# Second layer's convolution projection issued by token tile inside the combination of the first layer, with its weights and eight modulation pieces moved in the DMA queue

## The chip, the cores and the metric

The kernel runs on one core of a Trainium2 chip. The metric is the device time of one execution in microseconds (us); the time before is the median of three runs. A core has TensorE (PE in the profile, its weight loads PEld), VectorE (DVE), ScalarE (ACT), GpSimd (POOL) and SyncE (SP), which here issues nearly all large transfers; its queue is SPq. Each engine works through its own program in order, and they meet through semaphores.

## The reference, cut to what matters

Two layers of one trunk run on 640 tokens of 1024 float32 channels: 512 sample tokens and 128 prompt tokens, each group with its own conditioning vector. What touches the change:

```python
def adaln(cvec, w, b):                      # w is 1024 x 6144 for each layer
    m = jax.nn.silu(cvec) @ w + b
    return [part[:, None, :] for part in jnp.split(m, N_MOD, axis=-1)]

def trunk_layer(x, mods, n1, n2, mix_p, kf, attend, moe_p):
    sh1, sc1, g1, sh2, sc2, g2 = mods
    h = rmsnorm(x, n1) * (1 + sc1) + sh1
    y, k, v = token_mixers(h, *mix_p, kf, attend)   # h @ w_in, four mixers, @ w_out
    x = x + g1 * y
    h = rmsnorm(x, n2) * (1 + sc2) + sh2
    x = x + g2 * hier_moe(h, *moe_p)                # 32 experts, top 2 for each token
    return x, k, v
```

The first 512 columns of `w_in` feed the Conformer convolution: `a * sigmoid(g)` of the two halves, then a depthwise filter of 31 taps. Everything is float32.

## The kernel before, in words

**Tiles.** Tokens are cut into NT = 5 tiles of P = 128 (four of the sample, one of the prompt). `X` holds the tokens by row; `hT` holds the modulated, normalised tokens by channel, as KC = 8 blocks of 128 channels by 640 tokens. PSUM is `ps`, eight banks of 512 columns. Weights pass through `ring`, six slots of 1 MB; slots 0 to 3 are counted by `w_full`, slots 4 and 5 by `a_full`. Three more units of 1 MB, `inv_s`, `mix_s` and `fwd_s`, hold tables for the mixers and expert weights in the mixture.

**Order of a layer.** On PE: convolution projection (L1060 to L1094: four blocks of 128 output columns in the order 2, 0, 3, 1, each 8 matmul pairs, L1076 over the 512 sample tokens into bank m and L1077 over the 128 prompt tokens into bank 4), Fourier and attention projections, Hyena, then the output projection (L1310 to L1336: ten groups n = 0 to 9 of 8 matmuls of 512 columns at L1318, two for each token tile, with the transposes and the router of the tile before between them), routing, and the experts: NSTAT = 28 blocks in a written-out loop, then a loop of blocks that the router decides (`turns` turns of SLOTS = 2). A block is one expert on up to 64 rows: gather, gate and up (L1370), hidden (L1377), down (L1385), gate by DVE, scatter.

**Combination.** After the experts SP waits for the last scatters (L750) and reads the two expert rows of every token back from `y_scratch`, one transfer of 1 MB for each tile (the first in two halves, L755 to L758). DVE adds them to `X` (L2306, L2324, semaphore `x_new`). If a layer follows, ACT takes the sum of squares and the root (`statistics`, L1477 and L1479), DVE the reciprocal (`root`, L1806), ACT writes the scaled rows (`scaled_rows`, L1472), PE transposes them with 8 instructions (`columns_of_x`, L1031) and ACT and DVE modulate half of the blocks each into `hT` (`modulate`, L1487 and L1814). Before, PE does this for all five tiles (L1454 to L1461) and only then, with `h_act` and `h_dve` complete for the last tile, starts the convolution projection.

**Modulation pieces.** The product `silu(c) @ ada_w` comes in 24 pieces of 1 MB for each layer. `ada_piece(p)` is the transfer by SP (L579); `ada(p)` is PE's part, four matmuls of 512 columns into bank 5 (L940). `apos` gives the place of each piece; a transfer waits until the piece before it in the same place has been used (`a_free`, semaphore `a_used`). Eight pieces make a set; set 1 of the second layer is pieces 32 to 39. Its transfers 32 to 35 stand between those of the combination, 36 and 37 behind the convolution weights, 38 and 39 after the next two input weights; PE takes 32 to 37 between the tiles of the combination and 38 and 39 inside the projection. The result is read at the start of the second layer: ACT copies it (`ada_rows(1, 1)`, L1495), DVE adds the gate row (`gate_row`, L1832) behind the third tap of the convolution.

**After the projection.** ACT takes the sigmoid of blocks 2 and 3 (L1584 and, for the prompt tokens, L1590), DVE multiplies (L1954, L1957, semaphore `cv_glu`) and runs the 31 taps (L1972). PE goes on with the Fourier projection (L1103) when `cv_glu` is complete.

**SP's order around the change.** In the first layer: ... `gate_up_next(2)` after `a_used` reaches 32, wait for `wo_mm` 10 (the last group of the output projection), weights of the experts 0 and 1, then one gate/up and one down transfer for each block as its slot comes free; a loop for the blocks beyond the 28th; the combination's reads; `in_unit(1, 0)` and `in_unit(1, 1)` (L596), which are the two 1 MB halves of the second layer's convolution weights, into `ring` slots 0 and 1.

Of the kernel before, what the change touches and what calls it, by code (L numbers as in the profile page):

```python
# [12 lines left out]
P = 128  # L13
D = 1024
KC = D // P
# [84 lines left out]
def trunk(nc, io, out):  # L100
    ctx = ExitStack()
    with ctx:
# [150 lines left out]
        def kept(*dims):  # L253
# [212 lines left out]
            (cv_mm, 4), (cv_sig, 3), (cv_glu, 2), (cv_tap, 2 * TAPS),  # L466
# [24 lines left out]
        def w_count(l, j):  # L491
            return 16 * (2 + 3 * l + j // 4) + 16 * ((j % 4 == 3) * l + (j == OUT_U + 3)) + l * 32 * uses(0, gu_units, j % 4, NSTAT) \
                + 16 * l * apos[32:40].count(j % 4)
# [20 lines left out]
        def dn_count(l, n):  # L514
# [4 lines left out]
        apos = [(4, 5, 0, 1, 2, 3)[p] if p < 6 else (4, 6)[p % 2] if 24 <= p < 32 or p >= 40 else 2 + p % 2 if p in (34, 35)  # L519
                else 4 + p % 2 for p in range(24 * DEPTH)]  # L520
# [7 lines left out]
        def a_count(p):  # L528
            if p >= 32 and apos[p] < 4:
                return w_count(1, apos[p]) - 16 - 16 * apos[p:40].count(apos[p]) + 16  # L530
            return 16 * (len([n for n in range(p) if min(apos[n], 5) == min(apos[p], 5)]) + 1)
# [38 lines left out]
        def _(sp):  # L570
# [11 lines left out]
            def in_unit(l, j):  # L582
                lo, n, k0, k1 = {0: (0, 512, 0, 4), 1: (0, 512, 4, 8), 2: (1280, 256, 0, 8), 3: (1536, 512, 0, 4),
                                 4: (1536, 512, 4, 8), 5: (512, 256, 0, 8), 6: (768, 256, 0, 8), 7: (1024, 256, 0, 8)}[j]
                if j in (4, 5):
                    sp.wait_ge(cv_mm, nth(l, cv_mm, 4))
# [6 lines left out]
                elif j in (2, 3):  # L593
                    sp.wait_ge(a_used, 33 + j)
# [44 lines left out]
            for l in range(DEPTH):  # L639
# [7 lines left out]
                if l > 0:  # L647
                    ada_piece(38)
                    ada_piece(39)
# [63 lines left out]
                if l:  # L713
                    down_next(2)
                sp.wait_ge(wo_mm, nth(l, wo_mm, 10))
# [14 lines left out]
                for n in range(NSTAT + SLOTS - ahead_d):  # L730
# [6 lines left out]
                    down_next(n + ahead_d)  # L737
                with sp.Fori(1, turns) as j:
# [14 lines left out]
                for t in range(NT):  # L753
# [173 lines left out]
        def _(pe):  # L927
# [1425 lines left out]
```

## Time and profile before

| what | value |
|---|---|
| time of the runs | 1508.46, 1508.89, 1510.42 us; median 1508.89 us |
| span of the profiled execution, first to last instruction | 1502.3 us |
| its own time | not listed apart from the three; against the median 6.6 us lie around the span |
| PE busy | 1253.7 us, 83% of the span |
| DVE, ACT, POOL busy | 660.0, 330.3, 260.5 us |
| chain that ended last | PE 63%, DMA 15%, DVE 13%, issue 4%, ACT 3% |
| moved by DMA | 357.42 MB, mean 238 GB/s |
| mean granted clock of PE | 0.932 of full |

The span is what the instructions of the profile cover; the time of a run has the start and the end of the program around it. Times of rows are us from the span's start. "Busy" of PE is a modelled length of each matmul, of which neighbours overlap, so the distance between the starts of two rows says more than their lengths. A matmul in float32 appears as two instructions. The chain of waits follows the work that ended last back to what released it.

### The profile page before, as it was taken

Reading aid. Unit: us, or ns where it says so; the run is one execution under the profiler, and the core shown is the slowest. Engines: PE = TensorE matmul, PEld = TensorE weight load, DVE = VectorE, ACT = ScalarE, POOL = GpSimd, SP = SyncE. Lnnn points to the kernel's source line nnn. Section 1 sums busy time; section 2 is a strip of 40 time slices with the busy share of each in tenths; the row PEclk is TensorE's granted clock in tenths of the full one; section 3 lists DMA queues with packets and bytes.
Section 4 is the critical chain, followed back from the end, with each engine's and each line's share of the span. In section 5 each row is a group of like instructions: output and inputs, shape, how many; then the busy total and the mean of one; then the engine's idle time right before and its main releaser. Section 6 shows DMA issues by size and latency. Waiting matters only on the chain.

```text
span 1502.3 us, 17089 instructions
## 1 busy us (share of the span) xinstructions
PE 1253.7 (83%) x6582; PEld 733.0 (49%) x6582; DVE 660.0 (44%) x1402; ACT 330.3 (22%) x663; POOL 260.5 (17%) x265
## 2 busy tenths in 40 slices
PE   3899998988996889998873989898899688888871
PEld 1456474455554445554441466544645544444440
DVE  3327456365245443443335087454723533323235
ACT  4411124310431111111115011442023211111112
POOL 4210110001001233332320017000000023322220
PEclk9999999999995999999996999999999689999996
DMA  9747330063025999999978431214421669999985
GB/s 350 279 175 259 140 109 28 29 214 141 15 107 198 381 372 419 417 406 402 381 313 353 179 112 29 81 33 141 170 91 43 266 239 419 418 416 419 418 333 220
DMA packets 74099, 357.42 MB, mean 238 GB/s; under 512 B 13262, under 2 KB 22092, under 8 KB 38825
## 3 DMA queue, kind: packets, MB, share of 16 engines
q1 hardware_dynamic: 58588, 323.30, 55.5%
q0 software_dynamic: 12704, 22.03, 4.0%
q10 hardware_dynamic: 2732, 11.08, 1.9%
q8 instruction: 49, 0.80, 0.2%
q14 instruction: 26, 0.21, 0.0%
HBM read 339.27 MB, written 31.23 MB: 247 GB/s over the span
## 4 chain that ended last, share of the span: by engine, by line
PE 63%; DMA 15%; DVE 13%; issue 4%; ACT 3%; POOL 1%; SPq 1%; ACTq 0%; POOLq 0%; DVEq 0%
PE ps L1370 11%; PE ps L1318 9%; PE ps L1385 8%; PE ps L1171 5%; DMA work<-h_scratch,tabs 4%; PE ps L1076 4%; DMA ring<-in_ada_w 4%; PE ps L1132 3%; DMA mix_s<-in_exp_up 2%; PE ps L1103 2%; PE ps L940 2%; PE ps L1377 1%; PE ps L993 1%; DMA work<-y_scratch 1%; PE ps L1178 1%
## 5 line engine op out<-in xcount | busy, mean ns | idle before, releaser
L1370 PE MATMUL ps<-ring,work 128*64 128x256 f32 x1312 | 158.6, 397 | 5.0 <-DMA ring<-in_exp_up 3.4
L1385 PE MATMUL ps<-ring,work 128*64 128x512 f32 x456 | 122.6, 661 | 33.2 <-DVE work L2249 19.1
L1318 PE MATMUL ps<-ring,yT 128*128 128x512 f32 x320 | 140.3, 593 | 1.0 <-DVE yT L2095 1.0
L1370 PEld LDWEIGHTS ps<-ring,work 128*64 128x64 f32 x1312 | 102.6, 145 | 75.6 <-issue 31.5
L873 POOL DMA_INDIRECT y_scratch<-work,tabs x56 | 68.1, 1216 | 311.2 <-DVE work L2255 311.2
L868 POOL DMA_INDIRECT work<-h_scratch,tabs x60 | 62.5, 1041 | 304.8 <-DVE tabs L2229 279.1
L2255 DVE TENSOR_TENSOR work<-ps,yT 128x512 f32<-128x512 f32 x56 | 38.7, 691 | 141.0 <-PE ps L1385 141.0
L1972 DVE SCALAR_TENSOR_TENSOR work<-work,prmT 128x655 f32<-128x655 f32 x120 | 97.8, 894 | 0.0
L1318 PEld LDWEIGHTS ps<-ring,yT 128*128 128x128 f32 x320 | 59.5, 190 | 70.3 <-issue 68.4
L1171 PE MATMUL ps<-hT,ring 128*128 128x512 f32 x192 | 88.6, 604 | 1.1 <-DVE ring L1989 1.1
L1739 ACT ACTIVATE work<-ps 64x256 f32<-64x256 f32 x56 | 21.0, 375 | 298.7 <-PE ps L1370 298.6
L1370 PE MATMUL ps<-inv_s,work 128*64 128x256 f32 x320 | 72.4, 379 | 3.1 <-DMA mix_s<-in_exp_up 3.1
L1370 PE MATMUL ps<-mix_s,work 128*64 128x256 f32 x320 | 72.5, 380 | 0.0
L2247 DVE TENSOR_TENSOR work<-work,ps 64x256 f32<-64x256 f32 x56 | 23.8, 425 | 108.6 <-ACT work L1739 108.2
L1076 PE MATMUL ps<-hT,ring 128*128 128x512 f32 x128 | 67.4, 609 | 1.7 <-POOL hT L839 1.7
L1385 PEld LDWEIGHTS ps<-ring,work 128*64 128x64 f32 x456 | 30.5, 144 | 76.4 <-issue 45.4
L1731 ACT ACTIVATE work<-ps 128x512 f32<-128x512 f32 x70 | 41.8, 597 | 91.7 <-PE ps L1361 91.7
L940 PE MATMUL ps<-ring,c_act 128*32 128x512 f32 x320 | 47.0, 671 | 16.7 <-DMA ring<-in_ada_w 16.5
L1370 PEld LDWEIGHTS ps<-inv_s,work 128*64 128x64 f32 x320 | 43.9, 138 | 34.1 <-issue 16.4
L847 POOL TENSOR_TENSOR yT<-yT 128x512 f32<-128x512 f32 x4 | 31.7, 7923 | 162.5 <-ACT yT L1601 162.5
L1361 PE MATMUL ps<-sq,work 128*128 128x128 f32 x280 | 46.1, 288 | 13.3 <-DMA work<-h_scratch,tabs 11.9
L2103 DVE TENSOR_TENSOR work<-ps,work 128x512 f32<-128x512 f32 x20 | 13.8, 691 | 95.9 <-PE ps L1318 95.9
(386 smaller groups left out, 2050.4 us busy)
## 6 DMA issues: line engine op xcount, KB each, us to landing
ring<-in_exp_down SPq DMA_DIRECT2D x57, 1024.0 KB, 12.9
ring<-in_exp_gate SPq DMA_DIRECT2D x41, 1024.0 KB, 9.7
ring<-in_exp_up SPq DMA_DIRECT2D x41, 1024.0 KB, 14.1
ring<-in_ada_w SPq DMA_DIRECT2D x40, 1024.0 KB, 7.7
inv_s<-in_exp_gate SPq DMA_DIRECT2D x20, 1024.0 KB, 9.3
mix_s<-in_exp_up SPq DMA_DIRECT2D x20, 1024.0 KB, 15.0
ring<-in_w_in SPq DMA_DIRECT2D x16, 1024.0 KB, 8.4
fwd_s<-in_exp_down SPq DMA_DIRECT2D x11, 1024.0 KB, 18.6
```

The costliest lines, as they stand in the source:

```text
L868: pool.indirect_dma_start(xg[:, s, :], None, H_half, bass.IndirectOffsetOnAxis(ap=rows.bitcast(U32), axis=0), bounds_check=2 * T - 1, oob_ ...
L873: pool.indirect_dma_start(Y_half, bass.IndirectOffsetOnAxis(ap=rows.bitcast(U32), axis=0), ye[:, s, :], None, bounds_check=2 * T * TOPK - ...
L940: last = mm(ps[32 * g:32 * g + 32, 5, :], c_act[:, k, :], w[:, 512 * g:512 * g + 512], start=(k == 0), stop=(k == KC - 1))
L1076: mm(ps[:, m, :], lhs, hT[:, k, 0:LS], start=(k == 0), stop=(k == KC - 1))
L1132: mm(ps[:, bank, :], lhs, hT[:, k, 0:LS], start=(k == 0), stop=(k == KC - 1))
L1171: last = mm(ps[:, 7, :], wh[m // 2][:, k, m % 2 * P:(m % 2 + 1) * P], hT[:, k, 0:LS], start=(k == 0), stop=(k == KC - 1))
L1318: last = mm(ps[:, (4, 6, 7, 0)[n % 4], :], yT[:, k, t * P:(t + 1) * P], wo[k // 2][:, k % 2, h * HALF:(h + 1) * HALF], start=(k == 0), sto ...
L1361: last = tr(ps[:, 0, k * P:(k + 1) * P], xg[:, s, k * P:(k + 1) * P], ident)
L1370: last = mm(ps[BR * q:BR * q + BR, 1, 0:FE], xe[:, s, kb, BR * h:BR * h + BR], w[q][:, k, :], start=(k == 0), stop=(k == KC - 1))
L1385: last = mm(ps[BR * h:BR * h + BR, 3, :], he[:, s, k, :], wd[:, k, HALF * h:HALF * h + HALF], start=(k == 0), stop=(k == 1))
L1731: return A(xe[:, s, :, :], ps[:, 0, :].rearrange("p (k t) -> p k t", k=4), ACT.Copy)
L1972: V.scalar_tensor_tensor(out=acc[:, c, :], in0=glu[:, c, j:j + CONV], scalar=prmT[:, c, j:j + 1], in1=acc[:, c, :], op0=ALU.mult, op1=ALU. ...
```

## The change

The second layer's convolution projection is done by token tile. For each tile PE does the transposes, and after the transposes of the next tile the 32 products of that tile (4 blocks of output columns by 8 of channels) over 128 tokens each. The combination's transposes use banks 6 and 7 in place of 0 to 3. On ACT and DVE, modulation of a tile and its reciprocal stand in another order. The convolution weights are asked for before the loop of the blocks that the router decides. Pieces 32 to 39 are asked for when the first layer's Hyena output is complete (`hy_zn`) and used in the first layer's output projection, one behind each group 1 to 8. The routing weights' PSUM bank goes from 5 to 6, as bank 5 now holds the set. `cv_mm` counts to 5.

```diff
-        apos = [(4, 5, 0, 1, 2, 3)[p] if p < 6 else (4, 6)[p % 2] if 24 <= p < 32 or p >= 40 else 2 + p % 2 if p in (34, 35)
-                else 4 + p % 2 for p in range(24 * DEPTH)]
+        apos = [(4, 5, 0, 1, 2, 3)[p] if p < 6 else (4, 6)[p % 2] if 24 <= p < 32 or p >= 40 else 4 + p % 2 for p in range(24 * DEPTH)]
...
                 if j in (4, 5):
-                    sp.wait_ge(cv_mm, nth(l, cv_mm, 4))
+                    sp.wait_ge(cv_mm, nth(l, cv_mm, 5))
                 elif j == 6:
                     sp.wait_ge(fo_x, nth(l, fo_x, 5))
                 elif j == 7:
                     sp.wait_ge(at_mm, nth(l, at_mm, 5))
                 elif l == 0:
                     sp.wait_ge(a_used, 3 + j)
-                elif j in (2, 3):
-                    sp.wait_ge(a_used, 33 + j)
...
                 if l > 0:
-                    ada_piece(38)
-                    ada_piece(39)
                     table(mix_s, "mix_s", tab_in)
                     table(inv_s, "inv_s", tab_in)
...
                 gate_up_next(2)
                 if l:
                     down_next(2)
+                else:
+                    sp.wait_ge(hy_zn, nth(l, hy_zn, 4))
+                    for p in range(32, 40):
+                        ada_piece(p)
                 sp.wait_ge(wo_mm, nth(l, wo_mm, 10))
                 gate_up_next(0)
...
                     down_next(n + ahead_d)
+                if l + 1 < DEPTH:
+                    sp.wait_ge(g_mm, NSTAT)
+                    in_unit(l + 1, 0)
+                    in_unit(l + 1, 1)
                 with sp.Fori(1, turns) as j:
...
                     sp.dma_start(ycomb[t].rearrange("p k d -> p (k d)"), yrow[t]).then_inc(yc_in[t], 16)
-                    if l + 1 < DEPTH and t:
-                        ada_piece(31 + t)
-                if l + 1 < DEPTH:
-                    in_unit(l + 1, 0)
-                    in_unit(l + 1, 1)
-                    ada_piece(36)
-                    ada_piece(37)
...
+                wc = [wbuf(CONV_U + h, 4, 512) for h in range(2)]
+
+                def conv_tile(t):
+
+                    for n, m in enumerate((2, 0, 3, 1)):
+                        for k in range(KC):
+                            dst = ps[:, m, t * P:(t + 1) * P] if t < NT - 1 else ps[:, 4, m * P:(m + 1) * P]
+                            last = mm(dst, wc[k // 4][:, k % 4, m * P:(m + 1) * P], hT[:, k, t * P:(t + 1) * P],
+                                      start=(k == 0), stop=(k == KC - 1))
+                        if t == NT - 2 or t == NT - 1 and n == 3:
+                            last.then_inc(cv_mm, 1)
+
+                def tile_modulated(t):
+
+                    pe.wait_ge(h_act, norm_event(l, 0, t + 1))
+                    pe.wait_ge(h_dve, norm_event(l, 0, t + 1))
+
                 if l:
-                    pe.wait_ge(h_act, norm_event(l, 0, NT))
-                    pe.wait_ge(h_dve, norm_event(l, 0, NT))
+                    columns_of_x(l, 0, 0, (6, 7))
+                    pe.wait_ge(w_full[0], w_count(l, CONV_U))
+                    pe.wait_ge(w_full[1], w_count(l, CONV_U + 1))
+                    for t in range(1, NT):
+                        tile_modulated(t - 1)
+                        columns_of_x(l, 0, t, (6, 7))
+                        conv_tile(t - 1)
+                    tile_modulated(NT - 1)
+                    conv_tile(NT - 1)
                 else:
                     pe.wait_ge(mods_ok, 3)
-                pe.wait_ge(w_full[0], w_count(l, CONV_U))
-                pe.wait_ge(w_full[1], w_count(l, CONV_U + 1))
-                wc = [wbuf(CONV_U + h, 4, 512) for h in range(2)]
-                for c in range(2):
+                    pe.wait_ge(w_full[0], w_count(l, CONV_U))
...
-                            elif l and k == KC - 1 and place in (3, 7):
-                                ada(38 + place // 4)
...
                         if l and n == 0:
                             ada_columns(1, 2)
+                        if l == 0 and 1 <= n <= 8:
+                            ada(31 + n)
                         if h == 0 and t >= 1:
...
-                    for t in range(NT):
-                        e = norm_event(l + 1, 0, t)
-                        if t >= 2:
-                            pe.wait_ge(h_act, e - 1)
-                            pe.wait_ge(h_dve, e - 1)
-                        columns_of_x(l + 1, 0, t, ((0, 1), (2, 3))[t % 2])
-                        for p in ((), (32,), (33, 34), (35,), (36, 37))[t]:
-                            ada(p)
 
...
-                for t in range(NT + 2):
-                    if l + 1 < DEPTH and 1 <= t <= NT:
-                        scaled_rows(l + 1, 0, t - 1)
-                    if l + 1 < DEPTH and t >= 2:
-                        modulate(l + 1, 0, t - 2, (0, 2)[t % 2])
+                for t in range(NT + 1):
                     if t < NT:
                         act.wait_ge(x_new, nth(l, x_new, t + 1))
                         statistics(l + 1, 0, t, ycomb[t][:, 1, :])
+                    if l + 1 < DEPTH and t:
+                        modulate(l + 1, 0, t - 1, 6)
+                    if l + 1 < DEPTH and t < NT:
+                        scaled_rows(l + 1, 0, t)
 
...
-                    if l + 1 < DEPTH:
-                        if 1 <= t <= NT:
-                            root(l + 1, 0, t - 1).then_inc(st_dg, 1)
-                        if t >= 2:
-                            modulate(l + 1, 0, t - 2, (1, 3)[t % 2])
-                    elif t >= 2:
+                    if l + 1 == DEPTH and t >= 2:
...
                         V.tensor_tensor(X[:, t, :], X[:, t, :], ycomb[t][:, 1, :], ALU.add).then_inc(x_new, 1)
+                    if l + 1 < DEPTH and 1 <= t <= NT:
+                        modulate(l + 1, 0, t - 1, 7)
+                    if l + 1 < DEPTH and t < NT:
+                        root(l + 1, 0, t).then_inc(st_dg, 1)
```

## Rows read from the trace of the kernel before

**Rows 1.** The chain of waits, 780 to 960: start, length, what held it (times in us).
```profile
768.76 11.62 DMA mix_s<-in_exp_up
...
789.86 2.11 DMA y_scratch<-work,icol
...
795.95 14.83 DMA work<-y_scratch
...
815.55 14.26 DMA ring<-in_ada_w
...
831.79 1.74 PE ps L1076 x2
...
869.77 0.38 DVE work L1954
```

**Rows 2.** Busy time by stretch: PE, PEld, DVE, ACT, POOL, granted clock, DMA share, GB/s.
```profile
361.00:445.00 84.00, 83.28 (x292) 44.59 (x292) 25.76 (x73) 24.69 (x43) 6.10 (x12) 1.00 0.15 53
...
802.00:831.70 29.70, 17.31 (x88) 7.61 (x88) 15.36 (x39) 19.42 (x38) 0.00 (x0) 0.61 1.03 407
831.70:869.80 38.10, 37.97 (x148) 20.21 (x144) 0.72 (x2) 1.88 (x4) 0.00 (x0) 0.98 0.31 125
...
737.00:780.00 43.00, 34.52 (x238) 18.23 (x234) 13.60 (x30) 4.86 (x10) 11.82 (x20) 1.00 0.99 408
724.00:737.00 13.00, 11.28 (x88) 6.78 (x86) 5.17 (x12) 1.94 (x4) 4.74 (x8) 1.00 0.93 336
```

**Rows 3.** Instructions in order, 786 to 833: start, length, engine, line [idle before, releaser].
```profile
797.96 1.23 DVE L2324 TENSOR_TENSOR X<-X,work 128x1024 f32<-128x1024 f32 x1 [1.05 <-DMA work<-y_scratch]
...
800.40 0.29 ACT L1479 ACTIVATE stat<-stat,epsc 128x1 f32<-128x1 f32 x1
800.86 1.23 DVE L2306 TENSOR_TENSOR X<-X,work 128x1024 f32<-128x1024 f32 x1 [1.68 <-DMA work<-y_scratch]
...
802.20 1.15 ACT L1472 ACTIVATE work<-X,stat 128x1024 f32<-128x1024 f32 x1 [1.50 <-DVE stat L1806]
...
803.49 1.94 PE L1031 MATMUL ps<-sq,work 128*128 128x128 f32 x8 [15.53 <-ACT work L1472]
...
805.84 1.23 DVE L2306 TENSOR_TENSOR X<-X,work 128x1024 f32<-128x1024 f32 x1 [2.50 <-DMA work<-y_scratch]
...
808.23 1.48 ACT L1487 ACTIVATE hT<-ps,mods,gain 128x128 f32<-128x128 f32 x4
...
810.80 1.22 DVE L2306 TENSOR_TENSOR X<-X,work 128x1024 f32<-128x1024 f32 x1 [1.27 <-DMA work<-y_scratch]
...
815.77 1.23 DVE L2306 TENSOR_TENSOR X<-X,yT 128x1024 f32<-128x1024 f32 x1 [1.27 <-DMA yT<-y_scratch]
...
818.40 1.06 PE L1031 MATMUL ps<-sq,work 128*128 128x128 f32 x8 [2.04 <-DVE hT L1814]
...
824.51 1.36 DVE L1814 TENSOR_SCALAR hT<-ps,gain,mods 128x128 f32<-128x128 f32 x4 [2.04 <-PE ps L1031]
```

**Rows 4.** PE's instructions in order, first layer's output projection.
```profile
361.89 20.77 PE L1318 MATMUL ps<-ring,yT 128*128 128x512 f32 x48
```

**Rows 5.** PE's instructions in order, 838 to 843.7, old convolution projection.
```profile
840.08 1.02 PE L1076 MATMUL ps<-hT,ring 128*128 128x512 f32 x2
840.94 0.38 PE L1077 MATMUL ps<-hT,ring 128*128 128x128 f32 x2
841.25 1.07 PE L940 MATMUL ps<-ring,c_act 128*32 128x512 f32 x8
842.25 1.12 PE L1076 MATMUL ps<-hT,ring 128*128 128x512 f32 x2
```

**Rows 6.** Transfers issued from 750 to 1000: size, median us from issue to landing.
```profile
ring<-in_ada_w SPq DMA_DIRECT2D x9, 1024.0 KB, 13.5
```

**Rows 7.** SP's instructions in order, 655 to 800.
```profile
714.35 9.70 SPq L696 DMA_DIRECT2D ring<-in_exp_down  x2
```

**Rows 8.** Line L1139, second layer: duration in ns, first and last start.
```profile
L1139 PE MATMUL ps<-ring,hT x64: 275/275/276, 925.6 to 932.6; 128*128 128x128 f32 x64
```

More of the change, by code:

```diff
@@ L1060, in _ @@
             for l in range(DEPTH):
-                if l:
-                    pe.wait_ge(h_act, norm_event(l, 0, NT))
-                    pe.wait_ge(h_dve, norm_event(l, 0, NT))
+                wc = [wbuf(CONV_U + h, 4, 512) for h in range(2)]
[10 more added lines that the diff above has]
+                    pe.wait_ge(h_dve, norm_event(l, 0, t + 1))
+                if l:
+                    columns_of_x(l, 0, 0, (6, 7))
[7 more added lines that the diff above has]
+                    conv_tile(NT - 1)
                 else:
                     pe.wait_ge(mods_ok, 3)
-                pe.wait_ge(w_full[0], w_count(l, CONV_U))
-                pe.wait_ge(w_full[1], w_count(l, CONV_U + 1))
-                wc = [wbuf(CONV_U + h, 4, 512) for h in range(2)]
-                for c in range(2):
+                    pe.wait_ge(w_full[0], w_count(l, CONV_U))
+                    pe.wait_ge(w_full[1], w_count(l, CONV_U + 1))
+                for c in range(2 if l == 0 else 0):
                     for m in (2 + c, c):
                         for k in range(KC):
-                            if l == 0 and m == 2:
+                            if m == 2:
                                 pe.wait_ge(hm_act, k + 1)
@@ L1078, in _ @@
                             if k == KC - 1:
-                                last.then_inc(cv_mm, 1)
+                                last.then_inc(cv_mm, 1 + (m == 1))
                             place = 4 * (2 * c + (m < 2)) + k // 2
-                            if l == 0 and k % 2 and place == 0:
+                            if k % 2 and place == 0:
                                 filter_spectrum(0, 0, 1)
-                            elif l == 0 and k % 2 and place == 2:
+                            elif k % 2 and place == 2:
                                 filter_rest(0, 0)
-                            elif l == 0 and k % 2 and 0 <= place - 4 < NT:
+                            elif k % 2 and 0 <= place - 4 < NT:
                                 filter_rows(0, 1, place - 4)
-                            elif l == 0 and k % 2 and place in (10, 12):
+                            elif k % 2 and place in (10, 12):
                                 filter_spectrum(0, 1, place // 2 - 5)
-                            elif l == 0 and k % 2 and place == 14:
+                            elif k % 2 and place == 14:
                                 filter_rest(0, 1)
-                            if l == 0 and k % 4 == 3:
+                            if k % 4 == 3:
                                 ada(8 + place // 2)
-                            elif l and k == KC - 1 and place in (3, 7):
-                                ada(38 + place // 4)
                 if l == 0:
@@ L1349, in _ @@
                     for t in range(NT - 1):
[L1350 removed]
+                        mm(ps[:, 6, 0:NBLK + SLOTS], ohs[:, q * NT + t, :], ohw[:, q * NT + t, :],
                            start=(q + t == 0), stop=(q * NT + t == 2 * NT - 2))
                 for q in range(2):
[L1353 removed]
+                    last = mm(ps[:, 6, P:P + NBLK + SLOTS], ohs[:, q * NT + NT - 1, :], ohw[:, q * NT + NT - 1, :],
                               start=(q == 0), stop=(q == 1))
```

13 lines of the change are left out of this document (4 added, 9 removed).

## The prediction

> **What bounds the kernel now.** I read the chain of waits first, over the end of the first layer's experts and the start of the second layer. In [rows 1] the reader sees four owners in turn: the weights of the last blocks (a transfer of 11.62 us that PE waits for at 780), the combination's reads (from 795.95), then a modulation piece (14.26 us from 815.55), and from 831.79 the convolution projection, which ends at 869.77 where DVE takes over. So between 815 and 832 the kernel waits for eight transfers of 1 MB that the combination itself doesn't need, six pieces and two halves of the convolution weights. The table of stretches says the same [rows 2]: from 802 to 831.7 DMA is busy throughout (1.03, 407 GB/s) and PE only 17.31 of 29.7 us, at a mean granted clock of 0.61; in the 38.1 us behind it PE is busy for 37.97 and DMA for 0.31. PE waits for DMA, then DMA for PE. Two other stretches matter, since work is moved into them: in the first layer's output projection (361 to 445) PE is busy 83.28 of 84.00 us with DMA at 0.15, and in the loop of the last blocks (737 to 780) DMA is at 0.99 and 408 GB/s. Last I read the combination instruction by instruction [rows 3] for the pace of one tile.
>
> **Part 1: eight pieces go to the output projection.** PE first. PE issues the groups without a gap (the first three as one stretch of 20.77 us [rows 4], 6.9 each), so what is put between them lies on the path. The price of one `ada` among matmuls of 512 columns is in the old projection [rows 5]: from L1077 at 840.94 to the next L1076 at 842.25 are 1.31 us, where without it 0.22 stand (I take it as 1.08 for a pair of L1076 and L1077, 0.86 of which is L1076: 840.08 to 840.94); that is 1.09, and the next matmul is 0.10 longer (1.12 against 1.02). So 1.19 us, eight times, **+9.5 us**; the lower bound is the 1.00 from 841.25 to 842.25, eight times 8.0. The upper bound is a PE that also waits for the transfers. Pieces 32 and 33 are asked for when Hyena's output is complete, which is also what lets PE start group 0 at 361.89, and they stand behind the two transfers of block 2; the queue then holds 4 MB, 10 us at 2.49 us each (part 2), landing at 372 to 374. PE wants piece 32 behind group 1, at 361.9 + 2 x 6.9 = 375.7. From then on a piece is asked for when the one two before it is used, and wanted two groups later, some 15 us on; a piece landed in 13.5 us at the median where the queue was full [rows 6], and here it holds little else. SP stands in these waits only until group 6, and the next thing behind them, the weights of experts 0 and 1, waits for group 10 anyway; POOL's and ACT's queues aren't passed. Hidden margin about 2 us at the first piece, so zero for the transfers; if it were gone, each late us would cost one. The two pieces that leave the projection and the six that leave the combination are counted in part 3, where the whole stretch is worked out anew.
>
> **Part 2: two transfers before the loop of blocks.** SP has just waited for the 28th block's down (second transfer of the row at 714.35, so at 723.7 [rows 7]); the added wait for `g_mm` is already met. The two halves are 2 MB. The price of 1 MB on a full queue is read from the combination: tiles 2 and 3 were added to `X` at 805.84 and 810.80, two transfers apart, 2.49 us each [rows 3]; two cost 4.97. In the 13 us behind the insertion DMA has some room: 336 against 408 GB/s leaves 0.94 MB or 2.3 us; by its busy share of 0.93 only 0.9 us [rows 2]. Then it is full until 780 and PE waits for it at the end [rows 1]. So 2.7 to 4.1 us are left, and I take the middle, **+3.4**; bounds 0 (all absorbed) and 5.0 (none). What is queued behind: every later expert's weights, and behind those PE.
>
> **Part 3: the combination and the projection.** Times are on the clock of before, with the same end of the experts. Tile 0 is added at 797.96 + 1.23; ACT's sum and root end at 800.7 (800.40 + 0.29). DVE used to turn first to tile 1 (800.86 to 802.1) and then give the reciprocal; now it gives it at once, so the scaled rows start at 801.0 in place of 802.20 and PE transposes from 802.2 to 804.1 (1.94 us at the low clock). Tile 1, whose transfer keeps its place, is ready at 803.4; ACT takes sum and root until 804.9, modulates tile 0 until 806.4 (1.48), writes tile 1's rows until 807.6 (1.15), and PE transposes until 809.6. Here `conv_tile(0)` starts. All 32 of its products are 128 by 128 by 128. The value projection of the attention is of the very shape and operands: 64 instructions from 925.5 to 932.6 [rows 8], 0.112 us each or 7.15 us for one token tile, weight loads included. The work of PE is the same as before: four tiles of 128 make 512 columns, which took 0.86 us for a pair [rows 5], and five tiles are 35.8 us against 38.1 less two pieces. PE starts at the low clock: the old projection's first two instructions took 1.74 us where 0.86 is normal, although PE had worked on the last piece since its transfer ended at 829.8 [rows 1], and the transposes at 803.49 took 1.94 us, those at 818.40 1.06 [rows 3]. I charge 0.9 us (bounds 0 and 3). Then three more transposes of 1.0 and four tiles of 7.15: 809.6 + 8.1 + 3.0 + 28.6 = 849.3, against 869.77: **-20.4 us**. What could hold PE between tiles is the loop through DVE and ACT. For one tile ACT has 1.5 + 1.5 + 1.15 = 4.2 us and DVE 2 x 1.23 + 1.36 and a reciprocal, 4 us, both under PE's 8.2, and the tiles now land at 803.4, 805.8 and 808.3, since no piece stands between them (in place of 805.84, 810.80 and 815.77). Behind the projection everything depends as before: the sigmoid of the sample tokens runs under the last tile, the prompt's sigmoid (ACT) and product (DVE) come last; I cost it at nothing. The tables and the input weights 2 and 3, which waited for `a_used`, come earlier and under PE's work.
>
> The Trainium skill, in "TensorE: Matmul & The Clock Gate", Part 3 (what overlaps and what doesn't), says that a weight load overlaps matmuls in flight only when its row group differs. These loads use all rows, and the change issues 320 of them (two for each of the 160 products) where 128 stood, half of them behind products of 512 columns. The trace disagrees: in [rows 8] the starts are 0.112 us apart, no more than the products alone take by the 512-column row (0.43 for 512 is 0.108 for 128). By the rule's 128/1.2 ns for a load the sum would be an estimated 34 us longer.
>
> **Sum.** +9.5 + 3.4 - 20.4 = -7.5 us. The profiled execution has a span of 1502.3 us and, against the median of the runs, 6.6 us around it: 1508.9 - 7.5 = 1501.4 us. A change of 0.2%, 3 us, is about what a measurement of this kernel can tell from none.
>
> **The rivals.**
> A, the forecast, with a result between -3 and -11: 0.69.
> B, more is kept: the two transfers vanish in the queue's room, `ada` costs the 8.0 of its lower bound and PE is warm: 8.0 + 0 - 21.3 = -13.3. For it: PE's waits for weights are short before the last block. Against: a share of 0.99. Chance 0.12.
> C, less is gained: the clock stays low through `conv_tile(0)` and into the next (12 us at half speed cost 6, of which 0.9 is in the forecast) with the queue taking the full 5.0: 9.5 + 5.0 - 15.3 = -0.8. For it: a mean clock of 0.61 in this stretch. Against: that stretch had PE idle 12 us, the new one hardly. Chance 0.12.
> D, slower: weight loads aren't hidden. The place is `conv_tile`, 320 loads. Each exposed by x ns costs 0.32x us; the sign turns at 23 ns (7.5 / 0.32), and it is slower by over 0.2% from 33 ns. If the 0.108 us of a product's own length were added once more, +34.3 - 7.5 = +26.8, 1535.7 us. The rule of the Trainium skill named above would come out this way. Against it stands [rows 8]; for it only that here the PSUM region changes bank at every eighth product, as it doesn't there. Chance 0.03; with other ways to be slower (a piece late in the output projection, a gather of the experts behind the added 2 MB) 0.06.
> E, the change doesn't do what it says: PE reaches its first product only when the last tile is modulated. Before, that was at 825.9 (824.51 + 1.36), 10.1 us after tile 4 was there at 815.77 [rows 3]; with tile 4 at 808.3 it is 818.4, plus 35.8 and 1.7 for the low clock 855.9, or -13.9 in part 3 and -1.0 in the sum. Against it stands the order of the code, so 0.01; the number is worth having, as it says that two thirds of part 3 are the transfers that leave and one third is the tiling.
>
> **How the numbers follow.** The likeliest is 1501.4. The cases that aren't slower reach from -13.3 to -0.8, 1495.6 to 1508.1; the range leaves the last of C and D out above, and takes the ends 1495 and 1507. Faster by over 0.2%: A and nearly all of B, 0.81. Within: C and E, 0.13. Slower: 0.06.
>
> **What would show it.** The output projection of the first layer 8 to 9.5 us longer, with no idle time of PE before L940; the first block after the 28th and the last as far apart as before plus 3.4 (0 to 5); from the last scatter's end (789.86 + 2.11 before [rows 1]) to the end of the projection 57.3 us in place of 77.8; starts of the new projection's products 0.112 us apart; reads of the combination landing 2.5 us apart. It is wrong if PE waits in the output projection for pieces, if the granted clock is low after the first tile, or if the second layer behind the projection isn't as long as before.

## The result, and the profile after

| | before | changed |
|---|---|---|
| median of 8 runs | 1510.24 us | 1503.56 us |
| lowest and highest | 1507.41 to 1514.64 | 1500.37 to 1509.46 |
| ratio to before, 95% interval | | 0.996, 0.9942 to 0.9978 |
| profiled execution: span, its own time | 1502.3 us, not listed | 1500.6 us, 1502.39 us |

The change makes the kernel faster by 0.4%, 6.0 us by the ratio (3.3 to 8.8). The two spans show only 1.7 us of it. The changed kernel has 1.8 us between its span and its own time; if the first profile of before had the same, its execution took 1504.1 us and lay under everything in the first column, while I had put the whole 6.6 us around the span. A second profile of before, the first experiment, gives 1504.5 us of span and 1506.29 us of time: again 1.8. So spans of single executions aren't compared below; stages are, over several profiles.

In the profile after, the output projection comes first. PE's instructions in order, in the changed kernel (the columns as in [rows 4]):

```profile
363.16 13.90 PE L1332 MATMUL ps<-ring,yT 128*128 128x512 f32 x32
376.99 1.07 PE L933 MATMUL ps<-ring,c_act 128*32 128x512 f32 x8
377.99 7.13 PE L1332 MATMUL ps<-ring,yT 128*128 128x512 f32 x16
...
457.09 1.97 PE L1024 MATMUL ps<-sq,work 128*128 128x128 f32 x8 [1.78 <-ACT work L1480]
460.61 3.60 PE L1312 MATMUL ps<-wr,hT 128*128 128x36 f32 x16 [1.55 <-DVE hT L1822]
...
469.84 1.01 PE L1355 MATMUL ps<-route,sq 128*128 128x192 f32 x2 [3.88 <-DVE route L2148]
```

A piece (L933) stands behind each of the groups 1 to 8, with no idle time before it, and takes its 1.0 us and a little of the next group (7.13 for 7.03). From group 0 to the end of group 9 the stretch is 89.53 us; before it was 80.18. The last three rows are the surprise: transposes of 1.97 and a router product of 3.60 us, where the kernel before has, in the same view:

```profile
446.47 1.09 PE L1031 MATMUL ps<-sq,work 128*128 128x128 f32 x8 [1.79 <-ACT work L1472]
449.12 2.02 PE L1298 MATMUL ps<-wr,hT 128*128 128x36 f32 x16 [1.56 <-DVE hT L1814]
...
456.77 1.01 PE L1339 MATMUL ps<-route,sq 128*128 128x192 f32 x2 [3.87 <-DVE route L2140]
```

The busy time by stretch, in the changed kernel (columns as in [rows 2]): the output projection, 12 us behind it, the convolution projection.

```profile
363.20:452.50 89.30, 89.30 (x330) 42.12 (x329) 24.32 (x68) 23.15 (x39) 6.13 (x12) 1.00 0.38 137
456.70:468.70 12.00, 7.32 (x32) 6.55 (x32) 5.24 (x26) 6.81 (x10) 1.80 (x2) 0.51 1.01 399
...
826.60:866.20 39.60, 39.57 (x345) 39.38 (x343) 11.89 (x31) 14.93 (x28) 0.00 (x0) 0.97 0.23 88
```

PE is busy 89.30 of 89.30 us in the first. In the second its mean granted clock is 0.51, the lower of its two levels (1.2 GHz) nearly throughout. The last row is the old stretch of 38.1 us [rows 2] with the transposes of three tiles in it: PE busy 39.57 of 39.60 us.

The chain of waits over the same stretch as [rows 1] and somewhat ahead of it (start, length, what held it):

```profile
741.24 15.49 DMA ring<-in_exp_up
...
807.50 2.09 DMA y_scratch<-work,icol
...
810.60 7.51 DMA work<-y_scratch
...
824.70 1.94 PE ps L1024 x8
826.64 8.32 PE ps L1061 x64
...
851.87 14.31 PE ps L1061 x128
866.20 0.39 ACT work L1598
```

The modulation piece that held the chain for 14.26 us is gone, and so is half of the reads (14.83 us before, 7.51 here); from 826.64 the chain is PE alone. New is the first row: one transfer of expert weights that lands 15.49 us after it was asked for, where the longest before took 11.6 to 12.5. It stands directly behind the two transfers that were put there, and PE idles 5.34 us for it:

```profile
756.78 5.60 PE L1386 MATMUL ps<-ring,work 128*64 128x256 f32 x32 [5.34 <-DMA ring<-in_exp_up]
```

PE in the combination, in order:

```profile
818.86 1.94 PE L1024 MATMUL ps<-sq,work 128*128 128x128 f32 x8 [13.27 <-ACT work L1480]
824.70 1.94 PE L1024 MATMUL ps<-sq,work 128*128 128x128 f32 x8 [3.90 <-ACT work L1480]
826.44 8.53 PE L1061 MATMUL ps<-hT,ring 128*128 128x128 f32 x64
834.80 1.04 PE L1024 MATMUL ps<-sq,work 128*128 128x128 f32 x8
835.67 7.31 PE L1061 MATMUL ps<-hT,ring 128*128 128x128 f32 x64
...
851.71 14.46 PE L1061 MATMUL ps<-hT,ring 128*128 128x128 f32 x128
```

Each tile of the projection (L1061) starts 0.87 us after the transposes of the next one and takes 7.15 us; the first has 1.2 us more, at the low clock.

**Where the time went, by stage.** Stages end at marks that every profile has: start of group 0 and end of group 9 of the output projection, the rank product (L1339 before), down of the 28th block, down of the last block, first read of the combination, end of the projection. us; "before" is the two profiles of it. From the last down to the first read all of them have 6.1 us.

| stage | before | changed | difference |
|---|---|---|---|
| output projection | 80.18, 80.17 | 89.53 | +9.35 |
| group 9 to the rank product | 14.70, 14.62 | 17.15 | +2.5 |
| rank product to the 28th down | 263.5, 262.3 | 263.5 | +0.6 |
| 28th to last down | 65.8, 64.8 | 70.3 | +5.0 |
| first read to the end of the projection | 77.5, 78.8 | 56.4 | -21.7 |
| from there to the end | 632.6, 634.1 | 634.4 | +1.1 |

The sum of the four stages that the change touches is -4.9 us, inside the interval of the times (-3.3 to -8.8). The row of the experts and the last one differ by more among profiles of the same code than between the kernels.

### The profile page after: what moved, and what is told of

It is laid out like the page before. It is cut to its first block, busy times and chain, and to the rows that moved or that the text cites. A ratio compares the mean times of both kernels' runs of the same rounds, so it can differ in the third digit from the quotient of the medians.

```text
span 1500.6 us, 17475 instructions
## 1 busy us (share of the span) xinstructions
PE 1259.1 (84%) x6774; PEld 751.0 (50%) x6774; DVE 661.3 (44%) x1402; ACT 331.2 (22%) x663; POOL 260.9 (17%) x265
## 4 chain that ended last, share of the span: by engine, by line
PE 62%; DMA 17%; DVE 12%; issue 4%; ACT 3%; POOL 1%; SPq 0%; ACTq 0%; POOLq 0%; DVEq 0%
PE ps L1332 9%; PE ps L1386 9%; PE ps L1401 7%; PE ps L1185 5%; DMA ring<-in_exp_down 4%; DMA work<-h_scratch,tabs 4%; PE ps L1146 3%; PE ps L1061 2%; PE ps L933 2%; DMA ring<-in_ada_w 2%; PE ps L1117 2%; PE ps L1278 2%; PE ps L1092 2%; DMA mix_s<-in_exp_up 2%; PE ps L986 1%
## 5 line engine op out<-in xcount | busy, mean ns | idle before, releaser
L1401 PE MATMUL ps<-ring,work 128*64 128x512 f32 x456 | 125.8, 677 | 29.6 <-DVE work L2257 21.6
L1185 PE MATMUL ps<-hT,ring 128*128 128x512 f32 x192 | 88.6, 604 | 1.1 <-DVE ring L1997 1.1
L2255 DVE TENSOR_TENSOR work<-work,ps 64x256 f32<-64x256 f32 x56 | 23.8, 425 | 107.5 <-ACT work L1747 107.1
L1386 PEld LDWEIGHTS ps<-inv_s,work 128*64 128x64 f32 x320 | 44.0, 138 | 32.5 <-issue 13.6
L1377 PE MATMUL ps<-sq,work 128*128 128x128 f32 x280 | 46.1, 288 | 15.9 <-DMA work<-h_scratch,tabs 12.5
L1185 PEld LDWEIGHTS ps<-hT,ring 128*128 128x128 f32 x192 | 34.5, 189 | 43.8 <-issue 42.0
L933 PE MATMUL ps<-ring,c_act 128*32 128x512 f32 x320 | 43.7, 626 | 12.2 <-DMA ring<-in_ada_w 12.2
```

Of the source, the lines that this page charges most:

```text
L933: last = mm(ps[32 * g:32 * g + 32, 5, :], c_act[:, k, :], w[:, 512 * g:512 * g + 512], start=(k == 0), stop=(k == KC - 1))
L1185: last = mm(ps[:, 7, :], wh[m // 2][:, k, m % 2 * P:(m % 2 + 1) * P], hT[:, k, 0:LS], start=(k == 0), stop=(k == KC - 1))
L1377: last = tr(ps[:, 0, k * P:(k + 1) * P], xg[:, s, k * P:(k + 1) * P], ident)
L1386: last = mm(ps[BR * q:BR * q + BR, 1, 0:FE], xe[:, s, kb, BR * h:BR * h + BR], w[q][:, k, :], start=(k == 0), stop=(k == KC - 1))
L1401: last = mm(ps[BR * h:BR * h + BR, 3, :], he[:, s, k, :], wd[:, k, HALF * h:HALF * h + HALF], start=(k == 0), stop=(k == 1))
```

## The experiments

All are compared on one chip with the kernel before. Where nothing else is said, the edit is made on the changed kernel.

**The kernel before again.**

> The kernel before once more, for a second profile of it. Theory: the first profile of before (span 1502.3 us) lay some 5 us under its median, since the profile of the changed kernel has only 1.8 us between span and time; a second one should have a span of 1505 to 1510 us, and the stages around the change as in the first: 80.0 us from the start of the output projection's group 0 to the end of group 9, 77.6 us from the first read of the combination to the end of the projection. Rival: the 6.6 us lie around the span of this kernel, and the second span is again 1502 to 1504 us.

Median 1509.41 us, ratio 1.0 (0.9977 to 1.0023); span 1504.5, time 1506.29 us. The stage from group 0 to 9 is 80.17 us as in the first profile, that of the combination 78.8. The rival (6.6 us around the span) falls; by the same 1.8 us the first profile was of a quick execution.

**The convolution weights behind the reads.**

```diff
                     down_next(n + ahead_d)
-                if l + 1 < DEPTH:
-                    sp.wait_ge(g_mm, NSTAT)
-                    in_unit(l + 1, 0)
-                    in_unit(l + 1, 1)
...
                     sp.dma_start(ycomb[t].rearrange("p k d -> p (k d)"), yrow[t]).then_inc(yc_in[t], 16)
+                if l + 1 < DEPTH:
+                    in_unit(l + 1, 0)
+                    in_unit(l + 1, 1)
```

> The two transfers of the convolution weights stand behind the combination's reads again, all else as in the changed kernel. Theory: the 4.5 us that the loop of the last blocks has become longer are the price of these two transfers on a full queue; they go back (from the last written-out down to the last down 65.8 us as before, in place of 70.3), but the weights now land about 2.5 and 5.0 us behind tile 4, at some 21.5 us from the first read, and PE's first product, which stood at 16.9 us, waits 3.5 to 5 us for them. Total the same as the changed kernel within 1.5 us. Rival: the 4.5 us come from another alignment of the gathers, and stay: then 3 to 5 us slower than the changed kernel. Second rival: the weights come early enough, then 4 us faster.

1504.23 us, ratio 0.9974 (0.9955 to 0.9994): as the changed kernel. The last blocks' stage is 65.3 us, so the two transfers were the 5 us. PE in this run's combination:

```profile
817.18 1.94 PE L1023 MATMUL ps<-sq,work 128*128 128x128 f32 x8 [13.26 <-ACT work L1479]
830.08 1.94 PE L1023 MATMUL ps<-sq,work 128*128 128x128 f32 x8 [10.96 <-DMA ring<-in_w_in]
831.82 8.54 PE L1060 MATMUL ps<-hT,ring 128*128 128x128 f32 x64
```

The weights land at 830.0, 21.9 us behind the first read (808.11), as expected. The first product comes at 23.7 us and not at 20.4 to 22: PE's wait for the weights stands ahead of the transposes of tile 1, so 1.94 us of transposes, cold, come behind the wait. The stage is 63.5 us in place of 56.4. Of the 7.0 us by which the first product is later than in the changed kernel (16.7), the place of the wait is 1.8 (23.7 less 21.9) and the weights are the rest.

**The weights behind the loop of the last blocks.**

```diff
+                if l + 1 < DEPTH:
+                    in_unit(l + 1, 0)
+                    in_unit(l + 1, 1)
                 if l + 1 == DEPTH:
                     sp.dma_start(nfb, io["norm_f_g"].rearrange("(a d) -> a d", a=1).to_broadcast([P, D])).then_inc(tab_in, 16)
                 sp.wait_ge(k_out, 16 * 2 * DEPTH)
```

> The two transfers stand directly behind the loop of the last blocks and ahead of the wait for the scatters, where the queue runs empty (in the profile of before almost nothing moves between 780 and 794). Theory: the loop's stage is as long as before (65.8 us), and the weights land within the last block's compute, so PE's first product comes at 16.9 us from the first read as in the changed kernel: 4 to 4.5 us faster than the changed kernel, 10 to 11 faster than before. Rival: the two share the queue with the last block's three transfers and hold them up by up to 5 us: then as the changed kernel.

1499.69 us, ratio 0.994 (0.9917 to 0.9964), 4 us under the changed kernel by the medians and 3 by the ratios, whose intervals overlap; it is the stages that show the gain. SP, and below it PE, in this run:

```profile
783.08 0.33 SPq L688 DMA_DIRECT2D ring<-in_exp_down  x1
783.62 1.02 SPq L590 DMA_DIRECT2D ring<-in_w_in  x2
803.31 0.34 SPq L754 DMA_DIRECT2D work<-y_scratch  x1
```

```profile
818.25 1.94 PE L1023 MATMUL ps<-sq,work 128*128 128x128 f32 x8 [4.12 <-ACT work L1479]
819.98 8.93 PE L1060 MATMUL ps<-hT,ring 128*128 128x128 f32 x64
```

The two (L590) are issued 0.5 us behind the last block's down weights and 19.7 us ahead of the first read, and the last blocks' stage is 64.7 us. PE's first product stands 16.7 us behind the read, as in the changed kernel (16.7): the weights wait for PE. The rival falls; behind the last block's weights these two transfers delayed nothing.

**The projection whole, all else as changed.**

```diff
                     for t in range(1, NT):
                         tile_modulated(t - 1)
                         columns_of_x(l, 0, t, (6, 7))
-                        conv_tile(t - 1)
                     tile_modulated(NT - 1)
-                    conv_tile(NT - 1)
...
-                for c in range(2 if l == 0 else 0):
+                for c in range(2):
```

> The changed kernel, but PE does the second layer's convolution projection whole, behind the last tile, as before. Theory: two thirds of the gain in this stretch are the eight transfers that leave and one third is the tiling: from the first read to the end of the projection about 63 us, in place of 56.4 with tiles and 77.6 before; so some 6.6 us slower than the changed kernel, which is the time of before within 2 us. Rival: the tiling brings nothing, since PE's work is the same (56 to 58 us). Second rival: the tiling brings nearly all of it (above 70 us).

1518.12 us, ratio 1.0062 (1.0039 to 1.0086): slower than before, and the stage is 69.8 us. My theory said 63. PE in the combination:

```profile
818.63 1.94 PE L1024 MATMUL ps<-sq,work 128*128 128x128 f32 x8 [13.24 <-ACT work L1478]
823.90 1.94 PE L1024 MATMUL ps<-sq,work 128*128 128x128 f32 x8 [3.33 <-ACT work L1478]
828.65 1.94 PE L1024 MATMUL ps<-sq,work 128*128 128x128 f32 x8 [2.80 <-ACT work L1478]
833.79 1.94 PE L1024 MATMUL ps<-sq,work 128*128 128x128 f32 x8 [3.20 <-ACT work L1478]
838.53 1.94 PE L1024 MATMUL ps<-sq,yT 128*128 128x128 f32 x8 [2.80 <-ACT yT L1478]
842.02 2.05 PE L1090 MATMUL ps<-hT,ring 128*128 128x512 f32 x2 [1.55 <-DVE hT L1820]
```

The transposes (L1024) start 4.7 to 5.3 us apart, although the reads land 2.5 us apart, and PE idles 2.8 to 3.3 us before each, waiting for the scaled rows of ACT. DVE and ACT between the second and the third transposes:

```profile
825.88 1.36 DVE L1820 TENSOR_SCALAR hT<-ps,gain,mods 128x128 f32<-128x128 f32 x4 [1.46 <-PE ps L1024]
827.17 0.15 DVE L1812 RECIPROCAL stat<-stat 128x1 f32<-128x1 f32 x1
827.35 1.15 ACT L1478 ACTIVATE work<-X,stat 128x1024 f32<-128x1024 f32 x1
```

The change gave DVE and ACT another order. In it the reciprocal of a tile (L1812) stands behind the modulation of the tile before (L1820), which waits for that tile's transposes; so transposes, modulation, reciprocal and scaled rows follow one another, 4.75 us from 823.90 to 828.65, with no read in the round.

The tiles of before were held by something else. There DVE gave the reciprocal ahead of the modulation, and it waited 2.50, 1.27 and 1.27 us for the reads of tiles 2, 3 and 4, which start to be added 4.97 us apart [rows 3]. The last transposes, ahead of which DVE had no further read to wait for and no further rows to add, came 4.13 us after those at 818.40:

```profile
822.53 1.94 PE L1031 MATMUL ps<-sq,yT 128*128 128x128 f32 x8 [1.23 <-DVE hT L1814]
```

So the reads, with the pieces between them, did hold the old tiles, at 5 us each; when they left, the new order held them at nearly the same pace. The old order with the pieces gone was not run.

The first product comes at 842.02, 32.5 us behind the read, against 39.6 before, where it waited for two pieces. Of the 21.7 us, 8.4 (78.2, the mean of before, to 69.8) come with everything but the tiling: the transfers that leave and the new order together. The tiling adds 13.4, since PE's 36 us now run over these rounds instead of behind them. The shares are those of this order of steps, and not what either edit would bring alone.

**Four pieces moved behind the output projection.**

```diff
-                    for p in range(32, 40):
+                    for p in range(32, 38):
                         ada_piece(p)
...
-                        if l == 0 and 1 <= n <= 8:
+                        if l == 0 and 1 <= n <= 4:
                             ada(31 + n)
...
+                if l == 0:
+                    ada(36)
                 columns_of_x(l, 1, NT - 1, (7, 0))
+                if l == 0:
+                    ada(37)
                 router(NT - 1)
...
+                if l == 0:
+                    ada(38)
+                    ada(39)
                 pe.wait_ge(hs_ev, nth(l, hs_ev, 10))
```

SP asks for pieces 38 and 39 behind `gates_out(0, 1)`, and for the weights of expert 1 once `a_used` is 40.

> The changed kernel with PE's part of pieces 36 to 39 moved out of the output projection's groups into the idle time behind them: 36 ahead of the last transposes, 37 ahead of the last router product, 38 and 39 behind the rank product; transfers 38 and 39 and the weights of expert 1 follow. Theory: the eight parts lie wholly on the path (80.2 to 89.5 us from group 0 to group 9), so four fewer give 4.7 us back (84.8), and the four in the gaps cost nothing there, since PE idles 1.8, 1.6 and 5.2 us at these places; if they also keep the granted clock high, the 2.4 us that the stretch from group 9 to the rank product has become longer go too. 5 to 7 us faster than the changed kernel. Rival: behind group 9 the path runs through DVE and ACT, and any instruction of PE there delays the transposes: then the 4.7 us are only moved, and it is the same within 2 us.

1495.58 us, ratio 0.9897 (0.9871 to 0.9924): 8 us under the changed kernel, where 5 to 7 were expected. Output projection 84.85 us, group 9 to rank 14.62 us: 4.7 and 2.5 us given back. PE behind the output projection:

```profile
452.10 1.06 PE L941 MATMUL ps<-ring,c_act 128*32 128x512 f32 x8
...
454.97 1.06 PE L941 MATMUL ps<-ring,c_act 128*32 128x512 f32 x8
456.60 1.95 PE L1320 MATMUL ps<-wr,hT 128*128 128x36 f32 x16 [0.56 <-DVE hT L1837]
...
464.17 1.00 PE L1367 MATMUL ps<-route,sq 128*128 128x192 f32 x2 [4.73 <-DVE route L2163]
...
465.75 3.35 PE L941 MATMUL ps<-ring,c_act 128*32 128x512 f32 x16
```

Pieces 36, 37 (L941 at 452.10, 454.97) and the two at 465.75 stand where PE had waited, and the router product at 456.60 takes 1.95 us again. At 465.75 the clock is at the lower level and two pieces take 3.35 us, still under the wait for DVE.

**One matmul of four in each piece.** This leaves out three quarters of one set of modulation values, so the second layer computes other values and its router makes other blocks; only the first layer is read.

```diff
-                for g in range(4):
+                for g in range(1 if 32 <= p < 40 else 4):
```

> The changed kernel with one of the four matmuls of each of the pieces 32 to 39, so that three quarters of that set of modulation values are left out; all transfers stay. Theory: the output projection's 9.35 us more are PE's own work. A piece of one matmul is 2 instructions of 512 columns, 0.43 us or a little under, so the stretch is 80.2 + 8 x 0.45 = 83.8 us or a little more where the four matmuls of a piece run partly beside each other. Rival: the pieces' cost is a wait for their transfers or semaphores: then the stretch stays at 89.5.

The whole run is 1552.42 us (2.8% slower), with 678.9 us behind the projection in place of 634. The output projection is 89.37 us, so my 83.8 fell. PE in it:

```profile
384.06 1.05 PE L933 MATMUL ps<-ring,c_act 128*32 128x512 f32 x2
385.04 1.09 PE L1024 MATMUL ps<-sq,work 128*128 128x128 f32 x8
```

Two instructions take 1.05 us and the next starts 0.98 us on, nearly as with all eight (1.07 and 1.0). The four matmuls of a piece write four different sets of 32 partitions and run beside each other; leaving out three saves nothing. The number alone would have fitted the rival (a wait), but there is no idle time before any piece in this run or in the changed kernel.

**Idle time filled, pieces left in the groups.**

```diff
+                if l == 0:
+                    pe.wait_ge(x_mid, nth(l, x_mid, 15))
+                    mm(ps[:, 7, :], ident, hT[:, 0, 0:LS], start=True, stop=True)
                 columns_of_x(l, 1, NT - 1, (7, 0))
+                if l == 0:
+                    pe.wait_ge(x_mid, nth(l, x_mid, 20))
+                    mm(ps[:, 6, :], ident, hT[:, 0, 0:LS], start=True, stop=True)
                 router(NT - 1)
```

> The changed kernel with two products added in PE's idle time behind the output projection (128x512, result unused), one ahead of the last transposes and one ahead of the last router product, where the run with moved pieces had pieces 36 and 37; the pieces stay in the groups. It separates the two things which that run did at once. Theory: the stretch from group 9 to the rank product is 17.15 us instead of 14.7 because the granted clock falls to half at some 4.5 us behind group 9, before the last router product (3.60 us for 1.87) and not behind it; with PE busy in the two gaps the clock stays at full until behind the last transposes of h, and the stretch is 14.6 to 15.0 us with 89.5 us ahead of it: 2 to 2.5 us faster than the changed kernel. Rival: the stretch is long for another reason (a later store or table load): 17 us or more, by up to 1.8 us for the added work.

1500.12 us, ratio 0.9931 (0.9905 to 0.9957), 3.4 us under the changed kernel by the medians (the intervals overlap); output projection 89.52, group 9 to rank 14.63 us. PE:

```profile
455.92 1.02 PE L1351 MATMUL ps<-hT,sq 128*128 128x512 f32 x2
...
458.81 1.02 PE L1355 MATMUL ps<-hT,sq 128*128 128x512 f32 x2
460.52 1.95 PE L1312 MATMUL ps<-wr,hT 128*128 128x36 f32 x16 [0.69 <-DVE hT L1828]
...
468.10 1.01 PE L1361 MATMUL ps<-route,sq 128*128 128x192 f32 x2 [4.73 <-DVE route L2154]
```

With work that nobody uses (L1351, L1355) the router product is back at 1.95 us and the rank product 2.5 us nearer. PE's idle time here, and the clock that follows it, made the 2.5 us; the pieces need not leave the groups for that.

**Both edits**, the weights behind the loop and the four pieces behind the output projection, run twice.

> Two edits at once on the changed kernel: the convolution weights behind the loop of the last blocks (5.2 us shorter loop, measured alone as 1499.7 us), and pieces 36 to 39 in the idle time behind the output projection. Theory: the two stages lie one behind the other and don't share a resource, so the gains add: 4 + 5 to 7 us, 1493 to 1495 us, 15 to 17 us faster than before. Rival: the four pieces bring nothing (the rival of the run above): 1499 to 1500 us.

> The kernel with both edits once more, since its profile showed 66.9 us for the loop of the last blocks where the weights-behind-loop run had 64.7, for a second look at that stage and a closer time. Theory: 64.5 to 67 us in this stage against 70.3 in the changed kernel, 1489 to 1494 us. Rival: the moved pieces and weights disturb the experts and the stage is 68 us or more.

1491.47 us, ratio 0.9847 (0.9819 to 0.9876), then 1491.54 us, ratio 0.9876 (0.9853 to 0.9899). The last blocks' stage is 66.9 us in the first profile and 64.75 in the second, so the first was scatter, as far as two profiles tell. The theory had 1493 to 1495 us; the two medians lie 2 us under it. This is the fastest version, 12 us under the changed kernel by the medians (13 and 17 by the ratios).

**The stages over all profiles.** Where the code of a stage is the same its length can be compared over runs, us:

| stage | with | without |
|---|---|---|
| group 9 to the rank product; idle time of PE left empty behind groups with pieces | 17.15, 17.15, 17.15, 16.28, 16.28 | 14.70, 14.62 (before); 14.62, 14.62, 14.63, 14.63 (filled) |
| 28th to last down; the two transfers ahead of the loop | 70.3, 70.5, 70.25, 70.0, 70.4 | 65.8, 64.8, 65.3, 64.7, 66.9, 64.75 |
| first read to end of projection; tiles, weights there in time | 56.4, 56.8, 56.9, 57.1, 57.1, 56.9, 56.3 | 69.8 (whole) |

In the first row the two of 16.28 us are the run with the projection whole, whose code up to there is that of the changed kernel, and the run with one matmul of four. In both the transposes still take 1.09 us and the router product 3.60: the clock fell between them, and not ahead of both. So the cost of this stage is 1.6 to 2.5 us, and it varies with the same code.

## Why the prediction was right or wrong

The forecast was 1501.4 us, 7.5 less than before, as the sum of +9.5, +3.4 and -20.4. The sign and the case held: the median is 2.2 us above the forecast. The stages came to -4.9, so the sum was 2.6 us off. Costs were 4 us too small (2.5 that no term had and 1.5 in part 2), the gain 1.3 too small; that they partly cancel is luck.

**Part 1, the pieces (+9.5).** Measured +9.35. The price of a piece read between two products of the old projection, 1.19 us, was right (1.17), and so was zero for the transfers: the pieces landed in 4.8 us at the median, and PE had no idle time before any. What the step missed lies behind it. The forecast took everything behind group 9 as unchanged, but it is 2.5 us longer (1.6 in two of five profiles), because the granted clock falls there some 4.5 us earlier with respect to group 9: the mean from 4 to 6 us behind it is 0.56, where the kernel before has 1.00 until 8 us behind it and 0.69 from 8 to 10. PE had idled 1.8 us at this place in both. Filling the idle time with unused products restores 14.63 us and the router product's 1.95, which shows that the idle time and the clock behind it are the cause; why it falls earlier in one kernel than in the other, no run here shows.

**Part 2, the two transfers (+3.4).** Measured +4.9 (mean of five profiles with them less mean of six without), the full 4.97 of two transfers on a busy queue. The failed step is "in the 13 us behind the insertion DMA has some room". I read room out of 336 against 408 GB/s; the share of 0.93 said that the engines were busy. I put the low rate down to the small packets of gathers and scatters, which no run tests. Of the 0.9 us that the share left, next to nothing helped, since the weights of the third block behind the 28th were what PE waited for next (they landed 15.49 us after they were asked for, and PE idled 5.34), and that block's down is 30.8 us behind the 28th in place of 23.8; later blocks win some 2 us of that back.

**Part 3, combination and projection (-20.4).** Measured -21.7. PE's first product stood at 16.7 us behind the first read (17.5 by the forecast's clock, 809.6 less 792.14), and a tile took 7.15 us as the value projection's rows said, though those have the two operands the other way round (`hT` held and the weights streamed). The three later transposes took 0.87 us and not 1.0. The loop through DVE and ACT stayed under PE, but its length was argued wrongly: the forecast added up each engine's own work (4.2 and 4 us), and the round over PE, DVE and ACT is 4.7 to 5.3 with PE cold. Against PE's 8 us for a tile neither shows. The cold start cost 1.2 us against 0.9. Half of the missing 1.3 us is the scatter of before, 77.5 and 78.8; the forecast used the shorter.

**The rivals.** B had the queue and the pieces too cheap. C had the queue's full price right and the clock wrong: the cold start cost 1.2 us and not 6. D falls by the rows above, 64 instructions in 7.15 us: weight loads of all rows were covered. The Trainium skill ("TensorE: Matmul & The Clock Gate", Part 3, what overlaps and what doesn't), taken by that list alone, would have them wait for matmuls in the same row group, with the length that the same page gives for a load (LDWEIGHTS) an estimated 34 us more; this trace shows none of it. The paragraph ahead of that list (The mechanism) also lets a load go ahead into a background weight buffer, and the trace doesn't speak against that. E was worked out wrongly. It kept the 10.1 us that before lay between the last tile's read and the end of its modulation, and put that end at 818.4, 26.3 us behind the first read; the run with the projection whole starts its first product at 32.5. There the last tile doesn't wait for its read but for the rounds of the tiles before it, about 5 us each in the new order of DVE and ACT. That run was the largest miss, 8 us in the total, and it turns the shares round: 8.4 us without the tiling and 13.4 by it.

**Span and time.** That 6.6 us lie around the span was an assumption; 1.8 do. The predicted 1501.4 started from the median and so wasn't touched by it.

## What to carry to other kernels

A transfer that isn't urgent costs its full length ahead of a loop that waits for weights and nothing behind that loop's last request; the same 2 MB cost 5 us in one place and 0 in the other, and were in time in both. When a serial chain over tiles idles the matrix engine, taking away what holds it (here the reads, at 5 us for a tile) gives only as much as the next hold allows: work out the whole round from one tile to the next in the new order of every engine, and not each engine's own work, and look at the distance between tiles afterwards. Work moved into a full stretch of PE costs its length, and a short idle stretch right behind it, in which the next step waits for another engine, took the same work for nothing here (four pieces, 4.7 us) and kept the clock up.

## What wasn't expected of the hardware

- Four float32 matmuls of 512 columns, each on its own 32 columns of the array, take 1.07 us together, and one of them alone takes 1.05.
- The granted clock behind a full stretch of PE depended on short idle times: two products of 1 us, put into gaps of 1.8 and 1.6 us, made a chain of 17.15 us one of 14.63, and their own time was hidden. Left empty, the same gaps let the clock fall ahead of the last transposes in three profiles (17.15 us) and behind them in two (16.28).
